# FFN gate and up products with the high and low rows moved as one 512-column matmul, summed at the eviction

## What is computed

```python
h = rms_norm(x, norm2_g)                      # 256 x 1024
x = x + (silu(h @ w_gate) * (h @ w_up)) @ w_down   # hidden width 2816
```

## Time and profile before

| | us |
|---|---|
| runs | 1323.98, 1324.71, 1326.99 |
| median | 1324.71 |
| span of the profiled execution | 1324.2 |
| FFN: first gate matmul to the end of the span | 1133.8 to 1324.2 |
| of 1133.0 to 1324.2 (191.20): PE / PEld / DVE / ACT / POOL busy | 187.77 / 177.00 / 31.88 / 83.80 / 153.34 |

### The profile page before, as it was taken

The page is one execution under the profiler, slowest core; times in us unless marked ns, Lnnn a source line. Parts: engine busy times, 40 slices in busy tenths (PEclk is TensorE's granted clock), DMA queues, the critical chain, the costliest instruction groups (busy, mean ns, idle before and its releaser), DMA issues.

```text
span 1324.2 us, 16101 instructions
## 1 busy us (share of the span) xinstructions
PE 1178.5 (89%) x6088; PEld 840.0 (63%) x6088; DVE 715.8 (54%) x1452; ACT 577.7 (44%) x1269; POOL 845.9 (64%) x511
## 2 busy tenths in 40 slices
PE   7999999978987787788678777788999999999999
PEld 7987999973332333333233333333889999999998
DVE  5443154389776675857768576555789623311111
ACT  7486564434323222324322222224676375644442
POOL 7696578776645454444554445442987558788885
PEclk9999999999989998988998998899999999999999
DMA  8443446469999999999999999998543336555542
GB/s 270 147 160 127 138 166 207 159 259 426 425 426 425 426 425 426 426 425 427 425 425 426 426 425 426 427 425 329 185 164 127 126 126 196 167 191 184 186 159 96
DMA packets 130221, 381.81 MB, mean 288 GB/s; under 512 B 8544, under 2 KB 83296, under 8 KB 97376
## 3 DMA queue, kind: packets, MB, share of 16 engines
q0 software_dynamic: 36864, 268.45, 48.3%
q1 hardware_dynamic: 91808, 112.25, 25.4%
q10 hardware_dynamic: 1472, 0.09, 0.1%
HBM read 379.72 MB, written 1.05 MB: 288 GB/s over the span
## 4 chain that ended last, share of the span: by engine, by line
PE 57%; DMA 31%; DVE 7%; ACT 2%; POOL 2%; issue 1%; SPq 0%; DVEq 0%; ACTq 0%
PE ps L694 30%; DMA rows_w<-peer_rows_in,arena 30%; PE ps L967 9%; PE ps L723 6%; PE ps L1139 4%; DVE rows_w L2122 2%; PE ps L1092 2%; POOL rows_w L653 1%; PE ps L1041 1%; DMA ring<-w_in_in 1%; DVE arena L2122 1%; ACT wgt L1460 1%; PE ps L784 0%; PE ps L759 0%; PE ps L770 0%
## 5 line engine op out<-in xcount | busy, mean ns | idle before, releaser
L465 POOL TENSOR_TENSOR w_lo<-ring,w_hi 128x1024 fp32r<-128x1024 f32 x204 | 503.2, 2485 | 142.7 <-ACT w_hi L449 142.5
L967 PE MATMUL ps<-arena,diag 128*128 128x512 f32 x448 | 222.2, 646 | 85.3 <-ACT diag L1469 85.3
L967 PE MATMUL ps<-rows_w,diag 128*128 128x512 f32 x508 | 244.3, 630 | 33.6 <-ACT diag L1469 33.6
L449 ACT ACTIVATE w_hi<-ring 128x1024 fp32r<-128x1024 f32 x204 | 209.9, 1057 | 137.2 <-PE ps L694 98.6
L653 POOL DMA_INDIRECT arena<-peer_rows_in,arena x112 | 131.3, 1172 | 171.9 <-PE ps L967 156.6
L694 PE MATMUL ps<-hT_hi,w_hi 128*128 128x256 f32 x816 | 234.4, 287 | 3.7 <-POOL w_lo L465 3.7
L653 POOL DMA_INDIRECT rows_w<-peer_rows_in,arena x128 | 165.8, 1295 | 109.6 <-PE ps L967 96.6
L694 PE MATMUL ps<-hT_lo,w_hi 128*128 128x256 f32 x816 | 231.5, 284 | 0.0
L694 PE MATMUL ps<-hT_hi,w_lo 128*128 128x256 f32 x816 | 231.4, 284 | 0.0
L967 PEld LDWEIGHTS ps<-arena,diag 128*128 128x128 f32 x448 | 87.6, 203 | 215.8 <-ACT diag L1469 120.2
L2122 DVE CUSTOM_DVE_ANT_0 rows_w<-rows_w,arena 128x1024 f32<-128x1024 f32 x128 | 155.4, 1224 | 106.8 <-DMA rows_w<-peer_rows_in,arena 106.6
(11 more groups left out here) (419 smaller groups left out, 1743.2 us busy)
## 6 DMA issues: line engine op xcount, KB each, us to landing
ring<-w_in_in SPq DMA_DIRECT2D x45, 1024.0 KB, 5.0
ring<-w_ffn_gate_in SPq DMA_DIRECT2D x11, 1024.0 KB, 5.1
ring<-w_ffn_up_in SPq DMA_DIRECT2D x11, 1024.0 KB, 5.2
ring<-w_ffn_down_in SPq DMA_DIRECT2D x11, 1024.0 KB, 5.0
ring<-w_out_in SPq DMA_DIRECT2D x8, 1024.0 KB, 5.3
ring<-w_branch_attn_in SPq DMA_DIRECT2D x4, 1024.0 KB, 5.9
ring<-w_branch_mlstm_in SPq DMA_DIRECT2D x4, 1024.0 KB, 5.3
ring<-peer_w_query_in SPq DMA_DIRECT2D x4, 1024.0 KB, 5.3
```

The source lines that it names most:

```text
L449: act.activation(hi_of(n, u)[:, t, 0:cols], raw_half(n, g)[:, t, 0:cols], ACT.Copy).then_inc(sem("hi_ready"), 1)
L465: pool.tensor_tensor(lo_of(n, u)[:, t, 0:cols], raw_half(n, g)[:, t, 0:cols], hi_of(n, u)[:, t, 0:cols].bitcast(F32), ALU.subtract).then_i ...
L967: ins = pe.matmul(acc[:, c, :], diag[:, p % 4, :], pick_row(p % TOPK, D + c * CW, CW), start=False, stop=True, skip_group_check=True)
```

## The change

The two tensors `hT_lo` and `hT_hi` become one, `hT`, with the low rows at 0 and the high rows at 1 (the names stay as views). A new function `both_parts` takes the place of `split_half` for gate and up: for each t and j one matmul moves both parts of the rows (2 x 256 = 512 columns) against the high weight into a whole bank, and a second one moves the high rows (256 columns) against the low weight into the bank's second half. The first half of a bank then holds high weight by low rows, the second half high by high and low weight by high rows; what was one sum is the sum of the two halves. A half takes two banks (2g + j), so every gate half uses banks 0 and 1, every up half banks 2 and 3.

TensorE's waits follow: gate c waits for `gate_scaled` of chunk c - 1, up c for `hid_ready` of chunk c - 1. VectorE adds the two halves of the banks: three operations for the gate where there was one, and two more ahead of the product with the up sums.

```diff
-        hT_lo = sb("hT_lo", [P, KT, S], R32)
-        hT_hi = sb("hT_hi", [P, KT, S], R32)
+        hT = sb("hT", [P, 2, KT, S], R32)
+        hT_lo, hT_hi = hT[:, 0], hT[:, 1]
...
+        ups = hidden.take(2, S)
...
+            def both_parts(n, g, fresh):
+
+                for u, ts, _ in split_units(n, g):
+                    pe.wait_ge(sem("lo_ready"), u + 1)
+                    hi, lo = hi_of(n, u), lo_of(n, u)
+                    for t in range(ts.start, ts.stop):
+                        if fresh is not None:
+                            pe.wait_ge(sem("in_low"), fresh + max(t + 1, 2))
+                        for j in range(2):
+                            js = slice(j * P, (j + 1) * P)
+                            to = ps[:, 2 * g + j, :]
+                            pe.matmul(to, hi[:, t, js], hT[:, :, t, :], start=(t == 0), stop=False, skip_group_check=True)
+                            ins = pe.matmul(to[:, S:2 * S], lo[:, t, js], hT_hi[:, t, :], start=False, stop=(t == KT - 1), skip_group_check=True)
+                    ins.then_inc(sem("unit_used"), 1)
+
             for c, n in enumerate(ffn_chunk):
-                if c >= 2:
-                    pe.wait_ge(sem("hid_ready"), c - 1)
                 for g in range(2):
-                    split_half(n, g, False, ps[:, (2 * c + g) % 4, :], fresh=None if c or g else LOW_X4)
+                    if c and g:
+                        pe.wait_ge(sem("hid_ready"), c)
+                    elif c:
+                        pe.wait_ge(sem("gate_scaled"), c)
+                    both_parts(n, g, None if c or g else LOW_X4)
...
-                act.activation(hid_hi[:, c % 4, :, :], ps[:, (2 * c + 1) % 4, :].rearrange("p (a b) -> p a b", a=2), ACT.Copy).then_inc(sem("hid_hi"), 1)
+                act.activation(hid_hi[:, c % 4, :, :], ps[:, 2:4, 0:S], ACT.Copy).then_inc(sem("hid_hi"), 1)
...
-                up = ps[:, (2 * c + 1) % 4, :].rearrange("p (a b) -> p a b", a=2)
-                dve.tensor_tensor(x, ps[:, (2 * c) % 4, :].rearrange("p (a b) -> p a b", a=2), rbc.unsqueeze(1).broadcast_to([P, 2, S]),
-                                  ALU.mult).then_inc(sem("gate_scaled"), 1)
+                gate, up = ps[:, 0:2, :], ps[:, 2:4, 0:S]
+                link(dve.tensor_tensor(x, gate[:, :, 0:S], rbc.unsqueeze(1).broadcast_to([P, 2, S]), ALU.mult))
+                link(dve.tensor_tensor(gate[:, :, 0:S], gate[:, :, S:2 * S], rbc.unsqueeze(1).broadcast_to([P, 2, S]), ALU.mult))
+                dve.tensor_tensor(x, x, gate[:, :, 0:S], ALU.add).then_inc(sem("gate_scaled"), 1)
                 dve.wait_ge(sem("unit_used"), ffn_unit[c] + 4)
+                link(dve.tensor_copy(ups, ps[:, 2:4, S:2 * S]))
+                link(dve.tensor_tensor(up, up, ups, ALU.add))
                 dve.wait_ge(sem("silu_ready"), c + 1)
                 dve.tensor_tensor(up, x, up, ALU.mult).then_inc(sem("hid_sum"), 1)
```

## The result

The changed kernel takes 1330.27 us (median of 10 runs, 1326.54 to 1334.07) against 1325.88 for the kernel before in the same series (10 runs, 1323.98 to 1326.99): 1.0030 times the time, 95% interval 1.0021 to 1.0040, some 4 us slower. In a later series it took 1328.15 against 1326.04, 1.0015 (1.0006 to 1.0023). Forecast were 1323.8, within 1321.8 to 1327.6; both measured medians lie above that range.

A forecast was written before the change was run, and what follows sets the result against it. The prediction took TensorE alone to bound the FFN. From the median 1324.7 us it subtracted 4.4 for fewer matmuls and added 3.5 for the pause at gate 1, giving 1323.8 us, range 1321.8 to 1327.6.

The forecast's parts named there:

- What bounds the kernel: In the FFN TensorE alone sets the time, busy 187.77 of 191.20 us; matmul savings and pauses reach the end.
- The matmuls: Gate and up halves: 352 groups of three matmuls become two, 0.3598 to 0.3472 us each, gaining 4.4 us.
- C: Gate and up: the moving operand in two pieces costs a second matmul start; no gain, 1328.2 us, chance 0.06.
- The wait of gate 1: Gate 1 waits for gate 0's scaling, starting at 1148.60 instead of 1145.14: loss 3.46 us, once.
- The clock: Behind the pause at gate 1: forecast without a fall; a fall to 0.50 would cost 1.7 us, or 3.4.
- Rival B: The granted clock falls behind the pause at gate 1: 1325.5 us, up to 1327.2, chance 0.36.
- The hidden values: Behind an even chunk's up half: a chain of about 3.6 us, covered by a 5.56 us gate half, costs nothing.
- Silu: Silu's input comes 2.15 us after the gate half, not 0.69; ScalarE's work slips by 0.1 us at most.
- VectorE: Four more operations a chunk, 44 in all, some 31 us of an idling engine, at 0.70 us each.
- D: VectorE's new operations meet GpSimd at 2.4 us; pauses of 1.4 us at five places, 1334 us, chance 0.04.
- E: A gate or up group costs its columns and one start: gain 9.4 us, 1318.8 us, chance 0.05.
- The sum: Whole kernel: 1324.7 - 4.4 + 3.5 = 1323.8 us, with no fall of the clock, chance 0.45.

The follow-up runs named there:

- second: Changed kernel with the FFN's rows in their own tensor, high and low parts of a tile side by side (contiguous moving columns): 1329.36 us, 1.0025.
- fourth: Changed kernel with contiguous moving columns and free banks for chunk 1's gate and up: 1323.41 us, 0.9982 of the kernel before.
- The eighth: Changed kernel with free banks for chunk 1, plus both 512-column matmuls of each t ahead of both 256-column ones (the pairs): 1322.23 us, 0.9963.
- the fifth: Kernel before with one wait more: gate 1 on TensorE waits for the Silu of gate 0. 1330.96 us, 1.0031.
- first: Changed kernel measured again with no edit, in a later series: 1328.15 us against 1326.04 for the kernel before, 1.0015.

## Why the prediction was wrong

**What bounds the kernel** was right. TensorE's starts made the time; each nanosecond of a group came through, and so did the pause.

**The matmuls: the term was mis-sized.** The step took 0.2273 us for the 512 columns from the down halves, where 512 follows 512, and 0.1199 for the 256 columns from streams of 256, and added them. In the changed kernel a group takes 0.3533, not 0.3472: a gain of 2.3 us instead of 4.4. The measured 2.3 lies in the lower half of the bounds that I had given, nothing to 9.4; the reason that I had named (C, the operand in two pieces) is refuted by the second and fourth runs. The eighth gives 0.3481, the forecast's price to within 0.001. Against the 2.3 measured, the row's 0.0126 us for each removed matmul was 2.1 too high. By an estimate, the 2.5 ns that the Trainium skill gives for an isolated matmul ("TensorE: Matmul & The Clock Gate", section "Back-to-back issue gap") make 0.9 us in all, 1.4 too low. Neither price gives the usual 0.353 of widths in turn. The row's holds in the halves in the lower state (0.347) and nearly for the pairs, whose gain is 352 x (0.3598 - 0.3481) = 4.1. That an average over two states would come was in no term of the sum.

**The wait of gate 1** was right: 3.46 forecast, 3.45 measured, with the three operations where they were expected.

**The clock: this step failed.** I had the fall as a rival with 0.36, from four pauses of which two were followed by it, and made the forecast without it. In the four profiled executions with an idle pause of 3 us at this place (the changed kernel twice, the second run, the fifth) it fell three times, and cost 2.5, 1.5 and 1.4 us. A choice between two cases of almost equal weight was put as one number. The step also took 1.7 us as the usual price, from one stretch of low clock; in one of the three it lasted twice as long, 6.8 us. The trace that the prediction read had that too: behind the other of its two pauses with a fall (TensorE resumes at 580.90) the clock was low for 6.8 us. Rival B was forecast at 1325.5, up to 1327.2; with the smaller gain and the measured 1.4 to 2.5 it comes to 1328.4 to 1329.5, counted on the 1325.88 of the series, and outside the range. The Trainium skill's rule that a long enough idle time puts the clock back to half ("TensorE: Matmul & The Clock Gate", section "HAM oscillation — how this bites in real kernels") held in three of these four.

**The hidden values, Silu, VectorE, GpSimd** were right: no wait but the one, operations of 0.69 to 0.70 us, the chain behind an up half covered. Rivals D and E did not come. The hidden values of chunk 2 were ready at 1193.11, up 3 began at 1195.06: 1.95 us to spare where 1.9 was forecast. D's price was a poor stand-in whatever came: its 2.378 us is a mean over operations of 1024 columns, the new ones have 512, and operations of 512 columns with all operands in SBUF took from 0.68 to 2.90 us in that stage.

**The sum.** 1325.88 - 2.3 + 3.45 + 0 to 2.5 gives 1327.0 to 1329.5. Over the kernel before these are 1.15 to 3.65 us. The second series' 2.1 lies in that; the first series' 4.4 does not quite, though its interval, 2.8 to 5.3, reaches into it. The variation of the first 40 us is larger than the remaining 0.8 us, but no run assigns them to it. That variation also widened what one profile says: I compared a single median of three, 1324.71, that later series put at 1325.9 to 1327.0. A range around that median had to be moved by more than 1 us for this alone.

## What to carry to other kernels

Ask of every buffer that a change doubles in use whose reader is late the first time round, not only in the steady loop: here the loop had 1.9 us to spare in each chunk and lost nothing, and the first turn, whose reader waits for a value made on the way, lost more than all chunks gained. Two banks that were idle at that moment gave it back. Price a TensorE pause of some 3 us as its length plus, in three of four profiled executions here, 1.4 to 2.5 us of half clock; where it cannot be removed, filling it with unused matmuls is worth trying. And where fewer, wider matmuls are to bring the fixed cost of those removed (0.012 us here), group the widths, wide with wide and narrow with narrow: here that brought it in every half, the alternating order in some halves only.

## What the runs showed of the hardware

The granted clock fell to 0.50 where TensorE had been without a gap for over 10 us and then idle for 2.98 us (fifth run) or 3.2 us (changed kernel). It fell while TensorE was still idle or 0.3 us after it resumed, and stayed low for 3.4 us (first and fifth runs) or 6.8 us (first series) although the stream behind was dense.

At the start of the program TensorE can run at half its later rate while the windows print a granted clock of 1.00. In the kernel before and in the fifth run (count of matmuls in brackets, those under way at the edges included):

```profile
14.00:16.00 2.00, 2.00 (x19) 1.00 0.76 144
```

```profile
14.00:16.00 2.00, 2.00 (x11) 1.00 0.76 147
15.00:16.00 1.00, 1.00 (x7) 1.00 0.35 26
17.00:18.00 1.00, 1.00 (x10) 1.00 1.07 378
```

That 1.00 is no measurement. The trace's records of the clock begin at 10.14 us in the kernel before, at 16.61 in the fifth run and at 19.12 after, and a stretch without a record is printed as 1.00. In all nine profiled executions in which the 192 matmuls start before the first record, they are 0.234 to 0.239 us apart up to it and 0.125 to 0.126 behind it; in the four in which they start after it, they are 0.127 or 0.128 apart at once. So the start most likely ran at half clock too, though no record says so. It is worth up to 2 us, differs from execution to execution, and a comparison of two single traces can take it for an effect.

A pair of a 512-column and a 256-column matmul takes 0.3468 or 0.3532 us, with the same instructions at the same granted clock, 0.0064 us, some 15 cycles of 2.4 GHz, apart, and the higher value comes from every third pair taking 0.011 more; streams of 256 columns were at 0.1200 in every half looked at.
